# First two weight pieces in pass order, the fourth piece in halves, router weights fetched later

## What is computed

```python
h = x
for layer in range(DEPTH):
    y = _rmsnorm(h, norm_mix_g[layer])
    proj = y @ w_in[layer]      # columns: q,k,v,o of the mLSTM heads, i and f gates, q,k,v of the attention
    ...
    h = h + (mixed @ w_out[layer])
    y = _rmsnorm(h, norm_ffn_g[layer])
    if layer % 2 == 0:
        h = h + _swiglu(y, ffn_w_gate[j], ffn_w_up[j], ffn_w_down[j])
    else:
        logits = y @ w_router[j]          # top 2 of 8 experts
        ...
```

## Time and profile before

| | |
|---|---|
| median of 3 runs | 1421.18 us (1420.07 to 1421.37) |
| the profiled execution | 1420.79 us, its span in the trace 1419.0 us |
| PE busy | 1407.2 us, 99% of the span |
| DVE busy | 1140.3 us, 80% |
| ACT busy | 1006.6 us, 71% |
| DMA | 447.04 MB, mean 315 GB/s |

### The profile page before, as it was taken

One profiled execution on the slowest core, in us unless ns is written; L12 is line 12 of the kernel. 1 busy time (PEld: TensorE's weight loads), 2 busy tenths in 40 slices (PEclk: granted clock), 3 DMA queues, 4 the chain that ended last, 5 costly groups with the idle time before them and its releaser, 6 DMA issues.

```text
span 1419.0 us, 19052 instructions
## 1 busy us (share of the span) xinstructions
PE 1407.2 (99%) x7021; PEld 1185.6 (84%) x7021; DVE 1140.3 (80%) x853; ACT 1006.6 (71%) x866; POOL 155.7 (11%) x195
## 2 busy tenths in 40 slices
PE   9999999999999999999999999999999999999997
PEld 8988888889988888888888888888888888888886
DVE  6677544457587888888888988888888888888997
ACT  6877533455887777777777777777777777777775
POOL 2210000000101999400000000000000000002000
PEclk9999999999999999999999999999999999999999
DMA  9745655564544899999999999999999999999993
GB/s 354 267 152 191 215 199 178 176 196 153 182 148 142 324 393 397 387 395 385 366 391 386 366 384 391 379 362 386 380 369 392 392 369 383 391 381 375 394 395 137
DMA packets 188546, 447.04 MB, mean 315 GB/s; under 512 B 7736, under 2 KB 9920, under 8 KB 188496
## 3 DMA queue, kind: packets, MB, share of 16 engines
q1 hardware_dynamic: 184048, 431.12, 83.3%
q0 software_dynamic: 3440, 11.58, 2.2%
q10 hardware_dynamic: 1008, 3.67, 0.6%
HBM read 435.84 MB, written 10.49 MB: 315 GB/s over the span
## 4 chain that ended last, share of the span: by engine, by line
PE 95%; DVE 2%; ACT 1%; DMA 1%; issue 1%; SPq 0%; DVEq 0%; ACTq 0%
PE ps L1755 89%; PE ps L2272 2%; DMA h<-in_x_dram 1%; PE ps L2237 0%; ACT whi L708 0%; PE ps L1787 0%; PE ps L1990 0%; PE ps L2114 0%; PE ps L1879 0%; ACT y L733 0%; SPq L405 0%; PE ps L2241 0%; PE ps L2198 0%; PE ps L1776 0%; PE ps L1881 0%
## 5 line engine op out<-in xcount | busy, mean ns | idle before, releaser
L1168 DVE TENSOR_TENSOR wlo<-raw,whi 128x2048 fp32r<-128x2048 f32 x401 | 917.4, 2291 | 209.4 <-ACT whi L708 208.1
L708 ACT ACTIVATE whi<-raw 128x2048 fp32r<-128x2048 f32 x402 | 771.3, 1919 | 345.7 <-PE ps L1755 338.7
L1755 PE MATMUL ps<-whi,xT_hi 128*128 128x512 f32 (+1 forms) x1232 | 485.9, 394 | 0.3
L1755 PE MATMUL ps<-wlo,xT_hi 128*128 128x512 f32 (+1 forms) x1232 | 479.8, 389 | 0.0
L1755 PE MATMUL ps<-whi,xT_lo 128*128 128x512 f32 (+1 forms) x1232 | 478.7, 389 | 0.0
L1755 PEld LDWEIGHTS ps<-wlo,xT_hi 128*128 128x128 f32 x1232 | 231.2, 188 | 48.7
L1755 PEld LDWEIGHTS ps<-whi,xT_hi 128*128 128x128 f32 x1232 | 231.4, 188 | 46.5 <-issue 1.1
L1755 PEld LDWEIGHTS ps<-whi,xT_lo 128*128 128x128 f32 x1232 | 231.6, 188 | 45.0
L1755 PE MATMUL ps<-whi,hid_hi 128*128 128x512 f32 x536 | 210.2, 392 | 0.0
L1755 PE MATMUL ps<-wlo,hid_hi 128*128 128x512 f32 x536 | 208.8, 390 | 0.0
L1755 PE MATMUL ps<-whi,hid_lo 128*128 128x512 f32 x536 | 208.6, 389 | 0.0
(11 more groups left out here) (288 smaller groups left out, 898.5 us busy)
## 6 DMA issues: line engine op xcount, KB each, us to landing
raw<-in_moe_w_gate_dram SPq DMA_DIRECT2D x112, 1024.0 KB, 7.5
raw<-in_moe_w_up_dram SPq DMA_DIRECT2D x112, 1024.0 KB, 8.0
raw<-in_moe_w_down_dram SPq DMA_DIRECT2D x112, 1024.0 KB, 7.6
raw<-in_w_in_dram SPq DMA_DIRECT2D x25, 1024.0 KB, 5.7
raw<-in_ffn_w_gate_dram SPq DMA_DIRECT2D x10, 1024.0 KB, 5.1
raw<-in_ffn_w_up_dram SPq DMA_DIRECT2D x10, 1024.0 KB, 5.2
raw<-in_ffn_w_down_dram SPq DMA_DIRECT2D x10, 1024.0 KB, 4.9
raw<-in_w_out_dram SPq DMA_DIRECT2D x8, 1024.0 KB, 4.9
```

What stands on the lines that cost most here:

```text
L708: act.activation(whi[:, i % NSPLIT, :], raw[:, i % NRAW, :], ACT.Copy).then_inc(hi_ready, 1)
L1168: dve.tensor_tensor(wlo[:, i % NSPLIT, :], raw[:, i % NRAW, :], whi[:, i % NSPLIT, :].bitcast(F32), ALU.subtract).then_inc(lo_ready, 1)
L1755: ins = pe.matmul(acc, lhs, rhs, start=start and m == 0, stop=stop and m == 2, skip_group_check=True)
```

## The change

On SP, `wif` and `convp` go behind piece 3, `h` goes straight behind piece 2, and piece 3 is fetched in two halves. On ACT and DVE, piece 3 is split in two halves, behind the squares and the diagonals as before. On PE, all groups of pieces 0 and 1 go pass by pass, each pass waiting for what it reads alone, and pieces 2 and 3 share one function that waits for halves. On POOL, the router's weights are fetched behind the first gains, with a counter of their own. `keep_busy` gives 40 small matmuls in place of 42.

```diff
-BEFORE_X, BEFORE_CHOICE, BEFORE_SLOTS = 42, 24, 8
+BEFORE_X, BEFORE_CHOICE, BEFORE_SLOTS = 40, 24, 8
...
-                        if (l, b) != (0, 0) and (l, b, half) != (0, 1, 0):
+                        if l or b > KS:
                             cols(n + 2 * b + half, w_in[l], half, FIRST_COLUMN[b])
-                        if (l, b, half) == (0, 1, 0):
-                            for t in range(TT):
-                                sp.dma_start(h[:, t, :], x[0, t * P:(t + 1) * P, :]
-                                             ).then_inc(x_in[t], 16)
...
             first_rows_of(2, 2, 4, arrived[2])
+            for t in range(TT):
+                sp.dma_start(h[:, t, :], x[0, t * P:(t + 1) * P, :]).then_inc(x_in[t], 16)
+            first_rows_of(3, 0, 2, half_in[2])
+            first_rows_of(3, 2, 4, arrived[3])
             sp.dma_start(wif[:].rearrange("p l c -> p (l c)"), w_gates).then_inc(wif_in, 16)
             sp.dma_start(convp[:].rearrange("p c k -> p (c k)"), conv_columns).then_inc(convp_in, 16)
...
-            pool.dma_start(wr[:, 0:KC * E].rearrange("p (k e) -> p k e", k=KC),
-                           w_router[0].rearrange("(k p) e -> p k e", p=P)).then_inc(small_in, 16)
...
             gain(1, g_mlstm[0], g_sb[0])
+            pool.dma_start(wr[:, 0:KC * E].rearrange("p (k e) -> p k e", k=KC),
+                           w_router[0].rearrange("(k p) e -> p k e", p=P)).then_inc(router_in, 16)
...
                     act.wait_ge(wif_in, 16)
                     act.activation(wif_hi, wif[:], ACT.Copy).then_inc(wif_hi_ready, 1)
                     square(s, 0)
...
                     root(s, 1)
+                    act.wait_ge(half_in[2], 16)
+                    act.wait_ge(piece_used, 1)
+                    high_part(3, 0, 2 * FB, part_hi[2])
+                    act.wait_ge(arrived[3], 16)
+                    high_part(3, 2 * FB, PIECE, hi_ready)
...
                     token_diagonal(s)
+                    dve.wait_ge(part_hi[2], 2)
+                    low_part(3, 0, 2 * FB, part_lo[2])
+                    dve.wait_ge(hi_ready, 4)
+                    low_part(3, 2 * FB, PIECE, lo_ready)
...
+            def weights_of_group(parts, whole, i, k, c):
+
+                if (i, k) == (0, 0) and c % 2 == 0:
+                    pe.wait_ge(parts[0], c // 2 + 1)
+                elif (i, k) != (0, 0) and c == 0 and k < 3:
+                    pe.wait_ge(parts[i], k + 2 - i)
+                elif c == 0:
+                    pe.wait_ge(whole, i + 1)
+
+            def first_piece_out(i):
+
+                hi, lo = (v[:, i, :].rearrange("p (k n) -> p k n", k=4) for v in (whi, wlo))
+                for k in range(4):
+                    kk = 4 * i + k
+                    for m, (w, x) in enumerate(((hi, xT_hi), (hi, xT_lo), (lo, xT_hi))):
+                        if m == 0:
+                            pe.wait_ge(hT_hi_ready, kk + 1)
+                        elif m == 1:
+                            pe.wait_ge(hT_ready, kk + 1)
+                        for c in range(4):
+                            if m == 0:
+                                weights_of_group(part_hi, hi_ready, i, k, c)
+                            elif m == 2:
+                                weights_of_group(part_lo, lo_ready, i, k, c)
+                            ins = pe.matmul(ps[:, c // 2, 256 * (c % 2):256 * (c % 2) + 256],
+                                            w[:, k, c * P:(c + 1) * P], x[:, kk, :],
+                                            start=kk == 0 and m == 0 and c % 2 == 0,
+                                            stop=kk == KC - 1 and m == 2, skip_group_check=True)
+                ins.then_inc(piece_used, 1)
```

More of the change, by code:

```diff
@@ L231, in trunk @@
         small_in = sem("small_in")
+        router_in = sem("router_in")
         zero_ready = sem("zero_ready")
@@ L235, in trunk @@
         quarter_in = [sem("quarter_in0"), sem("quarter_in1"), sem("quarter_in2")]
-        half_in = [sem("half_in0"), sem("half_in1")]
+        half_in = [sem(f"half_in{i}") for i in range(3)]
         part_hi = [sem("part_hi0"), sem("part_hi1"), sem("part_hi2")]
@@ L687, in trunk @@
         CONSTS = 10
-        SMALL = 16 * 5
+        SMALL = 16 * 4
         @block.scalar
@@ L789, in high_part @@
                     def high_part(i, c0, c1, ready):
-                        act.activation(whi[:, i, c0:c1], raw[:, i, c0:c1], ACT.Copy).then_inc(ready, 1)
+                        act.activation(whi[:, i % NSPLIT, c0:c1], raw[:, i, c0:c1], ACT.Copy
+                                       ).then_inc(ready, 1)
                     act.wait_ge(xc_in[0], 16)
@@ L1805, in first_columns_out @@
             def first_columns_out(i, half, s):
-                if i > 2:
-                    pe.wait_ge(lo_ready, i + 1)
+                pe.wait_ge(lo_ready, i + 1)
                 hi, lo = (v[:, i % NSPLIT, :].rearrange("p (k n) -> p k n", k=4) for v in (whi, wlo))
                 for two in range(2):
[L1811 to L1817, removed]
-                    for c, k in order:
+                    for c, k in [(c, 2 * two + j) for c in range(4) for j in range(2)]:
@@ L1822, in first_columns_out @@
                             pe.wait_ge(hT_ready, 8 * s + kk + 1)
-                            if i < 2 and k < 3:
-                                pe.wait_ge(part_lo[i], k + 2 - i)
-                            elif i < 2:
-                                pe.wait_ge(lo_ready, i + 1)
                         ins = passes(acc, xT_hi[:, kk, :], xT_lo[:, kk, :],
                                      hi[:, k, c * P:(c + 1) * P], lo[:, k, c * P:(c + 1) * P],
-                                     start=half == 0 and k == 0 and c % 2 == 0 and i > 0,
+                                     start=half == 0 and k == 0 and c % 2 == 0,
                                      stop=half == 1 and k == 3, weights_move=False)
-                    if half == 0 and two == 0 and s:
+                    if half == 0 and two == 0:
                         for t in range(TT):
@@ L1834, in first_columns_out, with second_columns_out @@
                 ins.then_inc(piece_used, 1)
-            def second_columns_out(i, bank):
+            def second_columns_out(i, half, bank):
                 hi, lo = (v[:, i % NSPLIT, :].rearrange("p (k n) -> p k n", k=4) for v in (whi, wlo))
                 for two in range(2):
-                    pe.wait_ge((part_lo[2], lo_ready)[two], (1, i + 1)[two])
+                    if two == 0:
+                        pe.wait_ge(part_lo[2], half + 1)
+                    else:
+                        pe.wait_ge(lo_ready, i + 1)
                     for c in range(4):
@@ L1843, in second_columns_out @@
                         for k in (2 * two, 2 * two + 1):
-                            ins = passes(acc, xT_hi[:, k, :], xT_lo[:, k, :],
+                            kk = 4 * half + k
+                            ins = passes(acc, xT_hi[:, kk, :], xT_lo[:, kk, :],
                                          hi[:, k, c * P:(c + 1) * P], lo[:, k, c * P:(c + 1) * P],
-                                         start=k == 0 and c % 2 == 0, stop=False, weights_move=False)
+                                         start=half == 0 and k == 0 and c % 2 == 0,
+                                         stop=half == 1 and k == 3, weights_move=False)
                 ins.then_inc(piece_used, 1)
@@ L2029, in mixer @@
                         out_of = tokens_out if b in (VS, VM, OM) else columns_out
-                        if b == 0:
+                        if (l, b) == (0, 0):
+                            first_piece_out(i)
+                        elif b == 0:
                             first_columns_out(n + i, half, s)
-                        elif (l, i) == (0, 2):
-                            second_columns_out(n + i, 2)
+                        elif (l, b) == (0, KS):
+                            second_columns_out(i, half, 2)
                         else:
```

10 lines of the change are left out of this document (5 added, 5 removed).

## The result

| | before | after |
|---|---|---|
| median | 1420.71 us (1420.07 to 1421.37, 12 runs) | 1423.78 us (1422.85 to 1425.65, 12 runs) |
| the profiled execution | 1420.79 us, span 1419.0 us | 1425.37 us, span 1423.6 us |
| PE busy | 1407.2 us | 1409.6 us |

The ratio is 1.0023, with a 95% interval of 1.0016 to 1.0031: 3.1 us slower, a small loss, but one whose interval lies wholly above 1.

A forecast was written before the change was run, and what follows sets the result against it. PE bounds the kernel, busy 1407.2 us of a 1419.0 us span. From 1420.8 us, late gate weights add 2.5 (pass order and halves included) and the falling clock 1.5: 1424.8 us, range 1421.8 to 1426.2.

The forecast's parts named there:

- the case in which the clock falls: Likeliest case: late gate weights plus fallen clock, 1420.8 + 2.5 + 1.5 = 1424.8 us, range 1423.6 to 1426.2; chance 0.48.
- The gate weights: ACT waits for wif until 21.6, diagonals are ready at 26.6, PE begins piece 3 2.5 us later (+0.95 to +3.15).
- The straggler: A 16 KB instruction fetch holding one DMA engine 1.4 us, kept in wif's landing; without it 1421.8 us, chance 0.09.
- The standstill: PE, at 22.5 ahead of the scales, stands still 4.1 us until the diagonals are ready at 26.6.
- Pass order: On PE, pieces 1 and 2 end near 22.5 in place of 23.39, -0.85 us; piece 1 begins at about 11.0.
- the one on chunk 4: Chunk 4's high part, first of ACT's pair from 10.30, ready near 10.95, limits PE, which would be there at 10.8.
- Piece 3 in halves: ACT and DVE split piece 3 in halves; PE's 0.74 us wait goes only because PE comes later; wins nothing.
- The clock: The 4.1 us standstill may halve PE's clock for some 3 us from its restart: +1.5 us, ends 0.8 and 2.5.
- The two cases of the prediction: First, late gate weights and clock falls, 1424.8 us, chance 0.48; second, late gate weights and clock holds, 1423.3, chance 0.36.
- The router's weights: Fetched near 60 us, wanted beyond 440: nothing; the dip of about 0.4 us goes from wif's landing.
- Keys and what follows: DVE's shift of 2.7 against PE's 2.5 takes 0.2 us of the keys' 0.45 slack: nothing to pay, at most 0.3.
- The reckoning by half: After PE's restart, the loss is half of the time at the slow clock: half of 3 us, 1.5 us.

The follow-up runs named there:

- the filled wait: Changed kernel plus 54 small matmuls on zeros on PE between the third piece and the scales; 1422.84 us, 1.94 over before.
- the run above: Changed kernel with the router's weights fetched at their old place, among POOL's first transfers; 1425.69 us, ratio 1.0030.
- 62 small matmuls: Changed kernel with the router's weights fetched at their old place and 62 small matmuls on zeros on PE ahead of the scales; 1423.25 us, ratio 1.0020.
- the wait behind the roots: Changed kernel, same fetch order, but ACT takes wif behind the second root and DVE subtracts behind the diagonals; 1419.82 us, ratio 0.9995.
- The three kernels without the loss: Changed kernel with wif and convp ahead of the tokens (1419.93 us), wif between tokens and piece 3 (1419.49), or ACT's wif wait behind the roots (1419.82).

## Why the prediction was right

The time came at 1423.78, inside 1421.8 to 1426.2 and 1.0 us under the point of 1424.8. The mechanism was the one forecast, and it is shown from three sides: one edit makes the loss, and two different edits, moving the transfer or moving the wait, take it away. That the median came so near the point is in part luck, though: the point was the sum for the case in which the clock falls, the clock fell in only about half of the executions, and where it fell for long it cost 2.2 to 2.4 us and not 1.5. By its steps:

- **The gate weights.** Forecast: `wif` at 21.6, diagonals at 26.6, piece 3 2.5 us late. In the profile: 21.98, 26.82, and 2.8 us where the clock is left out (5.03 - 2.20, counted at the pair scores). (My sum for the landing added 7.56 us to 14.45, though they had been counted from 14.58; put right it gives 21.74.) PE's later start is no part of this delay, and no work of the change: it lay between 4.97 and 5.46 over the profiles, at 4.99, 5.06, 5.46 and 5.46 in the four that have the old number of small matmuls. The landing stays loose: in the executions profiled with `wif` behind piece 3 ACT took it up between 20.95 and 22.58, so the bounds of 20.05 to 22.25 were about right and a bit low at the upper end. In the median the part without the clock isn't known closely: the filled wait puts it at 1.9 us at most, the executions whose mean clock is that of before (below) at 2.6.
- **The straggler.** I kept 1.4 us for an instruction fetch, and the landing came near. In the profile after, a fetch of 16 KB began at 17.96 and took 1.09 us of one engine. In the kernel with `wif` right behind the tokens, the fetch began at 18.05, just behind the moment at which ACT took `wif` up (17.84), and the gain of 4.1 us is 1.4 more than the 2.7 that 1 MB takes at 387 GB/s. That fits a fetch that holds up what is queued behind it, but no run took the fetch away, so it stays argued.
- **The standstill** was 3.6 us, not 4.1, because PE was not as early as I had it.
- **Pass order.** This term was mis-sized: -0.85 forecast, -0.45 seen (17.95 in place of 18.40 us), and piece 1 began at 11.63, not 11.0. Over all profiles, pieces 0 to 2 took 17.7 to 18.4 us in the nine with pass order and 18.4 to 18.8 in the three without. The step that failed is the one on chunk 4, whose high part I had ready near 10.95. It was taken up by ACT at 10.86 rather than 10.30, with the same 0.45 us wait for the transfer. Alone the pass order is worth nothing, since the diagonals are late then.
- **Piece 3 in halves** wins nothing here, as forecast: the wait is gone because PE comes later. Apart from the late gate weights it is worth up to 0.7.
- **The clock.** I gave one price, 1.5 us, and a 0.48 chance against 0.36 that it holds. Both happen. In the profiled execution it cost 2.2, or 2.4 against the kernel with 54 small matmuls (from the scales to the pair scores 16.14 us in place of 13.70), for some 5.4 us at the slow clock from PE's restart on; I had taken 3. In the profile with the router's weights early the slow clock lasted 3.4 us, and by the same count cost 1.5 (15.24 in place of 13.70). So its price isn't one number. Of the 12 executions six have a mean clock of 0.998 or 0.999, as the kernel before has, and a median of 1423.3; six have 0.996 to 0.997 and a median of 1424.3. (The groups aren't sharp: one of the first six took 1424.54, and a mean of 0.998 may still hide a short fall, as in the profile with the router's weights early.) The two cases of the prediction, 1423.3 and 1424.8, are near these two groups, and the median lies between them. The span that I gave for the first case alone, 1423.6 to 1426.2, follows from none of my terms; their ends added up give 1422.6 to 1426.5.
- **The router's weights.** The prediction gave their place no price of its own but 0.4 us of `wif`'s landing. Fetched early they cost 1.7 us, with `wif` taken up 0.6 us later in the profile. So the step from the landing to the time was mis-sized. The likely reason is that a longer standstill makes the slow clock likelier (a mean of 0.997 or less in six of 8 executions, against six of 12), so that near this point 1 us of delay costs more than 1 us; how much of the 1.7 that is stays open.
- **Keys and what follows.** No wait at the keys, as forecast: `ksT` was ready at 40.6 for a PE that came at 43.10. With `wif` right behind the tokens, where PE isn't held up before, it did wait 0.25 us for `ksT`.

The Trainium skill, TensorE: Matmul & The Clock Gate, section Why this matters for your kernels, warns of gaps between bursts of matmuls. The runs agree for the gaps of 3.6 and 4.2 us, not in every execution, and a gap of 2.7 us left the clock at 1.00 in the one profile that has it. The reckoning by half, which the prediction took from the same page, stands in its section HAM oscillation — how this bites in real kernels; 2.2 to 2.4 us lost for 5.4 us at the slow clock, and 1.5 for 3.4, are a little under half.

## What to carry to other kernels

A small transfer is as late as everything ahead of it in its queue, and a wait for it stops all that the engine has behind it, needed or not: before moving a transfer back, find its wait and read what is queued behind it. Put the wait just ahead of the first work that needs the data; either remedy alone won back all of the loss here. And when a stall lands on PE, ask for a second price, the clock, which need not be proportional to the stall: fetching the router's weights late was worth 1.7 us here, with a standstill that was 0.6 us shorter in the profiles.

## What the runs showed of the hardware

- The fall of the clock has no fixed place. In the changed kernel's profile PE stopped at about 23.3 and the clock fell at about 25.5, before PE came back; with the router's weights early PE stopped at about 23.4 and the clock fell at about 28.2, 0.6 us after PE had begun again at 27.58 (0.58 in the slice 28 to 29, above). Why the same program keeps its clock in one execution and loses it in the next was not found.
- Small matmuls on zeros in the gap held the clock: it read 1.00 there in the profiles of all three kernels that had them, and none of their 31 executions had a mean below 0.998.
- The 32 KB of the router's weights, on another queue, seem to delay `wif`. In the profiles with `wif` behind piece 3, ACT took it up at 21.54, 22.23 and 22.58 with this fetch early, and at 20.95, 21.23, 21.24 and 21.96 with it late: 0.8 us apart in the mean, though the ranges overlap. At 387 GB/s the bytes alone would take 0.08 us. There is a dip with the fetch early (209 GB/s at 14.5 before, 252 at 15 to 16 in the run above), where the changed kernel has 402. It isn't `wif` and `convp` that make it: the kernel with these two ahead of the tokens and the router's weights late has 398 and 414 GB/s at 14 to 16.
- Single executions differ by a microsecond for another reason too: in three profiles (54 and 62 small matmuls, and the wait behind the roots) PE waited 0.6 to 1.0 us for one low part near 1320 us, in layer 1, which before and after don't show. The profile with `wif` right behind the tokens lost 0.8 us between 1025 and 1415 us, too, with no wait of PE named there. What makes these come was not looked into. They don't show in the mean clock, so they blur the two groups above.
- The kernel with the best median fetches `wif` right behind the tokens: 1419.49, 0.9992 of before, an interval that still touches 1. The three kernels without the loss lie 0.8 to 1.0 us under before, each with an interval that touches 1; so that is about what pass order, halves and the router's late fetch win together.
